# Softplus of the recurrence parameter moved from behind the first MLP's norm to behind the program's opening norm

## The reference, cut to what matters

```python
log_a = -RG_C * r * jax.nn.softplus(-a_param)      # RG_C = 8, r is the recurrence gate
a = jnp.exp(log_a)
mult = jnp.sqrt(-jnp.expm1(2.0 * log_a))
...
def sq_relu_mlp(h, w1, w2):
    z = jax.nn.relu(h @ w1)
    return (z * z) @ w2
```

## Time and profile before

| what | value |
| --- | --- |
| median of 3 runs | 1094.59 us (1092.65 to 1095.33) |
| profiled execution, device time | 1090.11 us |
| profiled execution, span | 1088.3 us |
| TensorE busy | 1045.9 us, 96% of the span |
| GpSimd, ScalarE, VectorE busy | 725.3, 547.5, 473.8 us |
| granted TensorE clock, mean | 0.998 |

### The profile page before, as it was taken

One profiled execution on the slowest core, in us unless ns is written; L12 is line 12 of the kernel. 1 busy time (PEld: TensorE's weight loads), 2 busy tenths in 40 slices (PEclk: granted clock), 3 DMA queues, 4 the chain that ended last, 5 costly groups with the idle time before them and its releaser, 6 DMA issues.

```text
span 1088.3 us, 20330 instructions
## 1 busy us (share of the span) xinstructions
PE 1045.9 (96%) x8580; PEld 866.2 (80%) x8580; DVE 473.8 (44%) x664; ACT 547.5 (50%) x876; POOL 725.3 (67%) x454
## 2 busy tenths in 40 slices
PE   9999999999999999999999999999999999999796
PEld 8888799999879869999996444589986787787665
DVE  2125275231447956312116538444467344223433
ACT  7548365444556856444532124221334368478744
POOL 6976559998867599988880005540327786998863
PEclk9999999999999999999999999999999999999999
DMA  9671445555546545555556334300004454543241
GB/s 366 230 253 48 154 155 194 187 182 193 185 147 202 184 155 185 186 191 191 182 189 213 115 109 162 116 4 4 4 18 145 166 202 140 200 168 134 86 159 45
DMA packets 45865, 167.31 MB, mean 154 GB/s; under 512 B 5616, under 2 KB 5872, under 8 KB 45456
## 3 DMA queue, kind: packets, MB, share of 16 engines
q1 hardware_dynamic: 43328, 156.97, 41.3%
q0 software_dynamic: 2448, 9.05, 2.6%
HBM read 164.95 MB, written 1.05 MB: 153 GB/s over the span
## 4 chain that ended last, share of the span: by engine, by line
PE 84%; ACT 7%; DVE 6%; issue 2%; DVEq 0%; ACTq 0%
PE psum L434 30%; PE psum L471 19%; PE psum L691 16%; PE psum L2217 5%; PE psum L446 3%; PE psum L2365 1%; PE psum L244 1%; ACT high_r L946 1%; PE psum L207 1%; PE psum L1957 1%; PE psum L2107 1%; PE psum L2117 1%; DVE arena L1483 1%; PE psum L219 1%; PE psum L2283 1%
## 5 line engine op out<-in xcount | busy, mean ns | idle before, releaser
L777 POOL TENSOR_TENSOR ring_r<-ring,high_r 128x512 fp32r<-128x512 f32 (+1 forms) x366 | 637.1, 1773 | 147.4 <-ACT high_r L946 133.9
L946 ACT CAST high_r<-ring 128x1024 fp32r<-128x1024 f32 x246 | 253.8, 1050 | 175.5 <-DMA ring<-w 175.4
L471 PE MATMUL psum<-x_high,high_r 128*128 128x256 f32 x640 | 182.4, 285 | 2.8 <-DVE x_low L308 2.8
L471 PE MATMUL psum<-x_low,high_r 128*128 128x256 f32 x640 | 181.1, 283 | 0.0
L471 PE MATMUL psum<-x_high,ring_r 128*128 128x256 f32 x640 | 181.1, 283 | 0.0
L663 DVE TENSOR_TENSOR arena<-arena 128x512 f32<-128x512 f32 x32 | 46.9, 1466 | 197.1 <-ACT arena L639 197.0
L471 PEld LDWEIGHTS psum<-x_high,high_r 128*128 128x128 f32 x640 | 122.7, 192 | 4.1 <-issue 3.5
L471 PEld LDWEIGHTS psum<-x_low,high_r 128*128 128x128 f32 x640 | 122.7, 192 | 0.6
L471 PEld LDWEIGHTS psum<-x_high,ring_r 128*128 128x128 f32 x640 | 122.7, 192 | 0.0
L434 PE MATMUL psum<-ring,arena 128*128 128x512 f32 x256 | 113.4, 596 | 2.1 <-DVE arena L1585 2.1
L434 PE MATMUL psum<-high_r,x_high 128*128 128x512 f32 x256 | 101.6, 397 | 2.6 <-DVE x_low L304 1.6
(11 more groups left out here) (344 smaller groups left out, 1801.0 us busy)
## 6 DMA issues: line engine op xcount, KB each, us to landing
ring<-w SPq DMA_DIRECT2D x288, 512.0 KB, 3.2
row<-rows POOLq DMA_DIRECT2D x14, 512.0 KB, 5.4
arena<-relt SPq DMA_DIRECT2D x2, 1536.0 KB, 11.2
h<-x SPq DMA_DIRECT2D x1, 1024.0 KB, 4.8
arena<-lora POOLq DMA_DIRECT2D x2, 512.0 KB, 9.2
out<-h SPq DMA_DIRECT2D x2, 512.0 KB, 2.6
con<-consts SPq DMA_DIRECT2D x1, 529.0 KB, 5.4
arena<-pT POOLq DMA_DIRECT2D x2, 256.0 KB, 3.3
```

Source lines behind the costliest of these rows:

```text
L471: ins = nc.tensor.matmul(out, a, b, start=(k == 0 and q == 0), stop=(k == KT - 1 and q == 2))
L777: ins = nc.gpsimd.tensor_tensor(low(m)[:, part], raw(m)[:, part], read(high(m))[:, part], ALU.subtract)
L946: nc.scalar.copy(high(m), raw(m)).then_inc(high_made, 1)
```

## The change

The softplus with its two constants and four copies moves, unchanged, to stand directly behind `rms(0)` on VectorE, ahead of `project_dve(0)`. Its two ScalarE steps move to stand behind `split_for(W_QKV)`, which casts pieces 4 to 9, and ahead of `project_act(0)`. (The diff on record shows the attention loop as moved; it is the block from `p_ = ...` to `decay_ready` that changes its place.)

```diff
@@ ScalarE
             moments(0)
 
             split_for(W_QKV)
+            act.wait_ge(decay_part, 1)
+            nc.scalar.activation(spt[1], spt[0], ACT.Exp, scale=-1.0).then_inc(decay_part, 1)
+            act.wait_ge(decay_part, 3)
+            nc.scalar.activation(spt[3], spt[2], ACT.Ln).then_inc(decay_part, 1)
             act.wait_ge(rstd_ready, 1)
             project_act(act, 0)
...
             evacuate_high(act, T_H1, (XH, c8("norm_mlp0")))
             moments(1)
 
-            act.wait_ge(decay_part, 1)
-            nc.scalar.activation(spt[1], spt[0], ACT.Exp, scale=-1.0).then_inc(decay_part, 1)
-            act.wait_ge(decay_part, 3)
-            nc.scalar.activation(spt[3], spt[2], ACT.Ln).then_inc(decay_part, 1)
             mlp_act(act, 0, split_until)
@@ VectorE
             rms(0)
+            p_ = c8("a_param")
+            settle(nc.vector.tensor_scalar(spt[1], p_, -1.0, None, ALU.mult))
+            nc.vector.tensor_tensor(spt[0], p_, spt[1], ALU.max).then_inc(decay_part, 1)
+            dve.wait_ge(decay_part, 2)
+            nc.vector.tensor_scalar(spt[2], spt[1], 1.0, None, ALU.add).then_inc(decay_part, 1)
+            dve.wait_ge(decay_part, 4)
+            settle(nc.vector.tensor_scalar(spt[2], spt[2], -1.0, None, ALU.add))
+            settle(nc.vector.tensor_scalar(spt[4], spt[2], 0.0, None, ALU.is_equal))
+            settle(nc.vector.tensor_tensor(spt[2], spt[2], spt[4], ALU.add))
+            settle(nc.vector.reciprocal(spt[2], spt[2]))
+            settle(nc.vector.tensor_tensor(spt[3], spt[3], spt[2], ALU.mult))
+            settle(nc.vector.tensor_tensor(spt[3], spt[3], spt[4], ALU.add))
+            settle(nc.vector.tensor_tensor(spt[3], spt[3], spt[1], ALU.mult))
+            settle(nc.vector.tensor_scalar(spt[4], p_, -1.0, 0.0, ALU.mult, ALU.max))
+            settle(nc.vector.tensor_tensor(spt[3], spt[3], spt[4], ALU.add))
+            settle(nc.vector.tensor_tensor(cb, c8("b_in_x"), c8("conv_w3"), ALU.mult))
+            nc.vector.tensor_tensor(cb, cb, c8("conv_b"), ALU.add).then_inc(cb_ready, 1)
+            nc.vector.tensor_scalar(half_ga, c8("b_ga"), 0.5, None, ALU.mult)
+            nc.vector.tensor_scalar(half_gx, c8("b_gx"), 0.5, None, ALU.mult)
+            nc.vector.tensor_scalar(sp8, spt[3], 4.0, None, ALU.mult)
+            nc.vector.tensor_scalar(nsp8, spt[3], -4.0, None, ALU.mult).then_inc(decay_ready, 1)
             project_dve(dve, 0)
...
             rms(1)
-            (the same 20 lines)
             add_part = mlp_dve(dve, settle, 0, 1)
```

More of the change, by code:

```diff
@@ L1426, in _ @@
             rms(1)
[L1428 to L1448, removed]
             add_part = mlp_dve(dve, settle, 0, 1)
```

## The result

The changed kernel takes 1105.69 us, median of 4 executions (1103.59 to 1109.14), against 1094.69 us for the kernel before (4 executions, 1092.65 to 1095.33). The ratio is 1.0105, with a 95% interval from 1.0077 to 1.0133. Forecast were 1106.8 us, 1.011 times the time before. The profiled execution took 1103.59 us with a span of 1101.8 us, 13.5 us more than before.

The account below looks back on a forecast made before the run. TensorE, busy for 96% of the span, was taken as the bound. Stall 11.1 plus clock 2.5 minus 1.4 recovered gave +12.2 us: 1094.59 to 1106.8 us, range of 8 in 10 1101.5 to 1109.5.

Parts of the forecast that it names:

- the softplus in its old place: At the MLP's start: only TensorE's last gap is the softplus's price; moving it gives back 1.4 us.
- the main term: In the opening: 14 small VectorE instructions each wait for a GpSimd instruction; TensorE stalls 11.1 us for the first projection.
- The rival that the last instructions pass together: Opening: softplus instructions without settle pass together; stall 6.4 us, sum +6 to +7.5, about 1101.5 us; chance 0.08.
- the one that VectorE isn't held: Opening: VectorE passes between GpSimd's instructions, no stall, 1.4 us saved, 1093.2 us; chance 0.07.
- The prediction's bound of some 44 us: Opening: GpSimd's run ends at 43.72 us, only bias fills follow, so the softplus cannot reach much beyond 44 us.
- ScalarE's part: Opening: two functions with table loads, some 3 us, lie in slack before TensorE needs the projection and cost nothing.
- The clock: Behind the new stall: the idle stretch ends at the 1.2 GHz level; the way back costs 2.5 us, bounds 0 and 3.
- The drain: ScalarE in the opening: the skill page's drain of about 1.38 us behind a table load; would add 0.2 us only.
- The spread: Whole kernel: 1 to 2 us between runs, coming on top of the bounds 1099.5 and 1107.7 us.

Follow-up runs that it names:

- the three versions above: Softplus behind attention, in the opening with PSUM operands, or split between opening and old place: medians 0.7 to 2.1 us under the kernel before.
- the run with 48 warm-up steps: Changed kernel plus 48 warm-up matmul steps on TensorE ahead of its wait for the first projection: 1102.89 us, ratio 1.0094.
- the one run where low parts did follow: Changed kernel with the first projection ahead of the softplus on VectorE: 1108.31 us, ratio 1.0120.
- the version with that part alone: Changed kernel with VectorE's first three instructions and ScalarE's two functions in the opening, VectorE's other 15 at the old place: 1091.19 us, ratio 0.9990.

## Why the prediction was right

**Where TensorE stands decides.** The prediction priced the softplus in its old place at 1.4 us, not at the 14 us that the chain shows. 1.6 us came back. The wait of L691 is gone in the changed kernel and in each of the three versions above.

**One small instruction for each of GpSimd's.** This is the main term. Fourteen were to sit from 27 to 44 us; they did from 28.3 to 44.6, ten of them at 1.2 to 1.3 us, and the wait was 11.2 us where 11.1 were forecast. Halving GpSimd's instruction took it to 5.5 us, doubling it left it at 11.4, and moving the operands took it to nothing. The rival that the last instructions pass together is refuted by L1413 to L1415, and the one that VectorE isn't held by the whole stretch. That the two figures agree so closely is in part luck, since errors cancelled in this term. VectorE sat through the fills too, which I had as harmless, and the softplus ended at 44.56 instead of 43.8 us. Against that, I had added 0.75 us for the projection behind it, but TensorE started 0.13 us behind the softplus's end. And TensorE could have begun its third chunk at 33.16 us, not at 33.40. A late start of the block cost nothing: ScalarE's casts ended 1.4 us later than in the trace of before, behind a wait of 1.3 us for a weight piece, and the logarithm ended at 28.25 instead of 26.85. In the run with 48 warm-up steps it ended at 26.69, near the forecast, and the softplus still ended with the fills, at 44.2 us:

```profile
42.01 2.20 DVE L1417 TENSOR_SCALAR small<-small 128x8 f32<-128x8 f32 x1
```

Luck too is that nothing followed the fills. In the kernel before twelve low parts did, from 44.59 us; in the changed kernel the next started at 51.09, since ScalarE's next cast stands behind a copy that waits for TensorE. The prediction's bound of some 44 us takes this for granted ("only fills of the bias follow"); in the one run where low parts did follow, the wait was 14.9 us.

**ScalarE's part** was forecast to cost nothing; the version with that part alone confirms it.

**The clock** was forecast at 2.5 us, with the opening's warm-up as the price of the way back. In the first trace of the changed kernel it was 1.3 to 1.4: the low level lasted about 2.8 us behind the stall instead of some 5 in the opening. In the second trace of the same kernel it lasted over 5 us and cost 2.4. The bounds of 0 and 3 held both; a single figure for this term can't be right for every execution.

**The drain** behind a table load, weighed and not taken in the prediction, is absent here too: load at 25.22 us, function at 26.52, next load at 26.75.

**The spread** was too small: I gave 1 to 2 us between executions. The changed kernel's run from 1101.76 to 1112.62 us in two comparisons, and those of before from 1088.47 to 1101.63. The difference was forecast as 12.2 us. It is 11.0 us between the medians of the first comparison and 12.9 in the second, which is what 11.2 for the stall, 1.4 or 2.5 for the clock and 1.6 back make within a microsecond; the spread between executions is larger than what is left. In the profiled pair it is 13.5, where the low stretch at the second block's start (1.7 us) and the longer wait in the convolution (0.7) made up for the 1.2 us too much in the clock's term. What decides which short wait is followed by a low stretch is open.

## What to carry to other kernels

Before moving small VectorE work to a place where VectorE is idle, look at what GpSimd does there. An instruction of 0.17 us costs a whole GpSimd instruction if it needs what the two share, and then it is the count of instructions that is paid, up to the end of GpSimd's run; either put one operand in PSUM, or pick a place where GpSimd rests. And read a long chain through a small engine against the matmul engine's own timeline before believing its length: here 14 us on the chain were worth 1.6.

## What the runs showed of the hardware that was not expected

- A fill (MEMSET, SBUF written only) on GpSimd broke the turn between the two engines: a VectorE `tensor_scalar` on 128 x 8 waited 11.98 us, through two fills and eight low parts, where it waits 1.31 us with the fill moved away. In one trace, and for SBUF-to-SBUF `tensor_scalar` alone; why is open.
- The granted clock went to 0.50 for stretches of 3 to some 20 us behind waits of 1 to 2 us in some executions and not in others, with the same instructions and waits of about the same length. Behind the same stall of 11 us it came back after about 2.8 us in one trace and after over 5 us in another. Over 67 executions of the kernel before the time changes by 0.7 us for each 0.001 of mean clock, and this sets how small a difference a comparison of this kernel can show.
